# Hybrid attention and HGRN2 encoder layer with MoE: the output projection of a prompt tile issued in sixteen half pieces, and the first mixing tile's operands loaded one stage earlier

## What is computed

```python
h = rmsnorm(x, ln1) * (1 + sc1) + sh1
qa, ka, va, qb, fb, ib, gb = split(h @ w_in)
oa = sliding-window attention(qa, ka, va, sinks)       # 8 heads of 64, 2 key/value heads, window 128, blocks of 64
S, ob = hgrn_scan(S0, qh, kb, ih, logf)                # 8 heads, state 64x64, gated recurrence in blocks
ob = rmsnorm(ob, o_norm) * silu(gb)
x = x + g1 * (concat(oa, ob) @ w_out)                  # output projection, 1024 x 1024
h2 = rmsnorm(x, ln2) * (1 + sc2) + sh2
x = x + g2 * moe(h2)                                   # router, top 2 of 16 experts
```

## Time and profile before

| | |
|---|---|
| median of 3 runs | 1406.37 us (1403.38 to 1411.02) |
| the profiled execution, its own time | 1410.54 us |
| its span, first to last instruction | 1408.5 us |
| mean granted TensorE clock | 0.893 |
| TensorE busy | 1238.9 us, 88% |
| VectorE, ScalarE, GpSimd busy | 737.7, 550.8, 365.7 us |
| mixing stage in the span | 436.8 to 820 us, about |

### The profile page before, as it was taken

How to read it: one execution, slowest core, us unless ns; L and a number is a source line. 1 busy time by engine, 2 the same in 40 slices (tenths; PEclk the granted TensorE clock), 3 DMA queues, 4 the chain that set the end, 5 groups by cost and what they waited for, 6 DMA issues and landing times. The chain is left out here.

```text
span 1408.5 us, 21648 instructions
## 1 busy us (share of the span) xinstructions
PE 1238.9 (88%) x7081; PEld 1022.5 (73%) x7082; DVE 737.7 (52%) x1066; ACT 550.8 (39%) x921; POOL 365.7 (26%) x419
## 2 busy tenths in 40 slices
PE   3789999999595999999999816999999999879964
PEld 1568889988464888888888715788887887668853
DVE  2553510342553666756666466552555585655851
ACT  3363421323322434444444203441444465444640
POOL 1000200122502433433433012233323332433222
PEclk8799999999666998989988956999999999989987
DMA  9626773512256323303321166387759889887864
GB/s 352 215 90 206 253 277 108 162 51 70 70 144 191 102 72 101 102 31 102 102 72 46 34 220 243 135 270 197 249 179 312 275 283 371 268 288 254 268 242 89
DMA packets 119430, 249.87 MB, mean 177 GB/s; under 512 B 17713, under 2 KB 47153, under 8 KB 116290
## 3 DMA queue, kind: packets, MB, share of 16 engines
q1 hardware_dynamic: 107266, 204.92, 41.9%
q0 software_dynamic: 12096, 44.05, 12.0%
HBM read 205.02 MB, written 43.93 MB: 177 GB/s over the span
## 5 line engine op out<-in xcount | busy, mean ns | idle before, releaser
L2106 PE MATMUL psum<-e_w_h,e_x_h 128*128 128x512 f32 x432 | 173.8, 402 | 30.5 <-DVE w_gu L2219 23.7
L2108 PE MATMUL psum<-e_w_h,e_x_l 128*128 128x512 f32 x432 | 171.0, 396 | 0.0
L2107 PE MATMUL psum<-w_gu,e_x_h 128*128 x432 | 170.6, 395 | 0.0
L2053 POOL DMA_INDIRECT out<-e_work,e_to x26 | 87.9, 3380 | 302.1 <-DVE e_work L2207 302.1
L2219 DVE TENSOR_TENSOR w_gu<-w_gu,e_w_h 128x1024 f32 x128 | 146.7, 1217 | 21.1 <-ACT e_w_h L2160 21.1
L2160 ACT ACTIVATE e_w_h<-w_gu 128x1024 fp32r x128 | 123.0, 1048 | 54.5 <-issue 33.3
L2106 PEld LDWEIGHTS psum<-e_w_h,e_x_h 128*128 128x128 f32 x432 | 82.8, 192 | 48.7 <-DVE w_gu L2219 24.1
L498 PE MATMUL psum<-p_w_h,p_h_h 128*128 128x512 f32 (+1 forms) x288 | 107.4, 373 | 1.6 <-DVE p_h_l L653 1.6
L500 PE MATMUL psum<-p_w_h,p_h_l 128*128 128x512 f32 (+1 forms) x288 | 106.8, 371 | 0.0
L499 PE MATMUL psum<-p_w_l,p_h_h 128*128 128x512 f32 (+1 forms) x288 | 106.7, 371 | 0.0
L2108 PEld LDWEIGHTS psum<-e_w_h,e_x_l 128*128 128x128 f32 x432 | 82.5, 191 | 17.8
(11 more groups left out here) (367 smaller groups left out, 2661.5 us busy)
## 6 DMA issues: line engine op xcount, KB each, us to landing
w_gu<-in_w_e_gate SPq DMA_DIRECT2D x16, 2048.0 KB, 15.4
w_gu<-in_w_e_up SPq DMA_DIRECT2D x16, 2048.0 KB, 19.3
w_dn<-in_w_e_down SPq DMA_DIRECT2D x16, 2048.0 KB, 15.5
shared<-in_w_ada SPq DMA_DIRECT2D x24, 1024.0 KB, 6.6
p_w_raw<-in_w_in SPq DMA_DIRECT2D x5, 2048.0 KB, 9.3
m_feat<-feat_d SPq DMA_DIRECT2D x8, 1024.0 KB, 6.6
m_tok<-tok_d SPq DMA_DIRECT2D x8, 896.0 KB, 8.9
tok_d<-p_tok SPq DMA_DIRECT2D x27, 256.0 KB, 2.0
```

The lines of the kernel that those rows point to most:

```text
L2053: pool.indirect_dma_start(out=d["y"], out_offset=bass.IndirectOffsetOnAxis(ap=to_now[1 - par][:, 0:1], axis=0), in_=y_s[:, 1 - par, :], in ...
L2106: pe.matmul(psum[:, j, :], x_h[:, k, :], wh, start=(k == 0), stop=False)
L2107: pe.matmul(psum[:, j, :], x_h[:, k, :], wl, start=False, stop=False)
L2108: last = pe.matmul(psum[:, j, :], x_l[:, k, :], wh, start=False, stop=(k == KC - 1))
```

## The change

1. `fill(u, k)` is cut into `piece(u, k, 0)` and `piece(u, k, 1)`, three matmuls of 512 columns each. In a tile the steps 0 and 1 are still whole; the twelve others are single halves between other steps: two of them now stand in the end of the tile (before and behind `pair`), one between `scores(t, 1)` and level 3, one between the logits and `values(t, 0)`. `values(t, 1)` moves ahead of step 6.
2. `feat` and `tok` have their first buffer (`feat0`, `tok0`) in the memory that lives through both stages; `sampling` loads tile 0 into it, ahead of its wait for the new state. `mixing` no longer does. To make room, `pn_t` and `o_sq` of `sampling` become parts of `cache_t` and `kd_tok`.

```diff
--- before.py
+++ after.py
@@ -167,7 +167,8 @@
             b["w_ol"] = nc.alloc_sbuf_tensor_at("w_ol", [P, KC, D], F32R, offset=low_at)
             b.update(
                 mix_p=sb(mid, "mix_p", [P, 2, KC, P]), w_oh=sb(mid, "w_oh", [P, KC, D], F32R),
-                w_r=sb(mid, "w_r", [P, KC, NE]))
+                w_r=sb(mid, "w_r", [P, KC, NE]), feat0=sb(mid, "feat0", [P, 4, QW]), tok0=sb(mid, "tok0", [P, TOK]),
+                feat0_loaded=sem("feat0_loaded"), tok0_loaded=sem("tok0_loaded"))
             sampling(nc, b, d, sinks, state_in, s_sample)
             mixing(nc, b, d, x, sinks, s_prompt)
         b.update(
@@ -718,6 +719,17 @@
 OUT_A, OUT_B, M0, M1, M2, M3, PJ0, PJ1 = range(8)
 
 
+def load_feat(sp, d, t, feat, loaded):
+
+    sp.dma_start(feat[:, :, :].rearrange("p a (c r) -> p (a c) r", r=P),
+                 d["feat"][:, :, :, t * P:(t + 1) * P].rearrange("p a c r -> p (a c) r")).then_inc(loaded, 16)
+
+
+def load_tok(sp, d, t, tok, loaded):
+
+    sp.dma_start(tok[:, :], d["tok"][t * P:(t + 1) * P, :]).then_inc(loaded, 16)
+
+
 def sampling(nc, b, d, sinks, state_in, s_sample):
 
 
@@ -756,7 +768,7 @@
         top_s, neg_top, sink_e = (sb(n, [P, NKV, BP]) for n in ("top_s", "neg_top", "sink_e"))
         den, rec = sb("den", [P, NKV, BP]), sb("rec", [P, NKV, BP])
         pc_t = sb("pc_t", [P, 8, P])
-        pn_t = sb("pn_t", [L, 8, P])
+        pn_t = cache_t[0:L, :, :]
         o_a = sb("o_a", [P, BP, NKV, HD])
         exp_b, k_d, kd_tok, o_n = (sb(n, [P, QW]) for n in "exp_b k_d kd_tok o_n".split())
         gap = sb("gap", [P, NL, QW])
@@ -769,7 +781,7 @@
         q_m = sb("q_m", [P, 4, NB * (P + L)])
         i_m = sb("i_m", [P, 8, NB, HD])
         new_state = i_m[:, 0:4, :, :]
-        o_sq = sb("o_sq", [P, 8, HD])
+        o_sq = kd_tok[:, :].rearrange("p (h d) -> p h d", d=HD)
         o_ss, o_rs = sb("o_ss", [P, 8]), sb("o_rs", [P, 8])
 
         names = """gate_loaded sink_loaded state_loaded vnew_loaded consts act_chain dve_chain pool_chain
@@ -811,6 +823,8 @@
             for half in (slice(0, D // 2), slice(D // 2, D)):
                 sp.dma_start(d["h2"][ROWS:TABLE, half], zeros[:, :]).then_inc(s["operands_in"], 16)
                 sp.dma_start(d["y"][ROWS:TABLE, half], zeros[:, :]).then_inc(s["operands_in"], 16)
+            load_feat(sp, d, 0, b["feat0"], b["feat0_loaded"])
+            load_tok(sp, d, 0, b["tok0"], b["tok0_loaded"])
             sp.wait_ge(s["state_ready"], 1)
             for n in range(NB):
                 for h in range(2):
@@ -1111,7 +1125,7 @@
 
         w_h, w_l, w_r, mix_p = b["w_oh"], b["w_ol"], b["w_r"], b["mix_p"]
         table = b["shared"][:, :].rearrange("p (a i n) -> p a i n", a=3, i=2)
-        feat, tok = sb("feat", [P, 2, 4, QW]), sb("tok", [P, 2, TOK])
+        feat, tok = (b["feat0"], sb("feat1", [P, 4, QW])), (b["tok0"], sb("tok1", [P, TOK]))
         x_in, x2 = sb("x_in", [P, 2, D]), sb("x2", [P, 2, D])
         xw, h2, h2_t = sb("xw", [P, D]), sb("h2", [P, D]), sb("h2_t", [P, KC, P])
         lhs_h, lhs_l = sb("lhs_h", [P, KC, P], F32R), sb("lhs_l", [P, KC, P], F32R)
@@ -1143,8 +1157,8 @@
             lhs_h_ready lhs_ready lhs_used x1_ready x2_ready squared rs_ready xw_ready h2_ready h2_stored h2_turned h2t_ready
             logit_mm logit_ready""".split()
         s = {n: sem(n) for n in names}
-        feat_loaded, tok_loaded, x_loaded, x2_stored = ([sem(f"{n}{i}") for i in range(2)]
-                                                        for n in ("feat_loaded", "tok_loaded", "x_loaded", "x2_stored"))
+        x_loaded, x2_stored = ([sem(f"{n}{i}") for i in range(2)] for n in ("x_loaded", "x2_stored"))
+        feat_loaded, tok_loaded = (b["feat0_loaded"], sem("feat1_loaded")), (b["tok0_loaded"], sem("tok1_loaded"))
         ctx.callback(retire, nc, sems)
         block = ctx.enter_context(nc.Block())
 
@@ -1166,10 +1180,10 @@
             return mix_p[:, (u + 1) % 2, part, :]
 
         def fts(t, i):
-            return feat[:, t % 2, i, :]
+            return feat[t % 2][:, i, :]
 
         def toks(t, a, n):
-            return tok[:, t % 2, a:a + n]
+            return tok[t % 2][:, a:a + n]
 
         def table_row(i, u):
             return table[:, i, tile_of(u) // TP, :]
@@ -1181,12 +1195,11 @@
                     sp.wait_ge(s["lv_mm"], 2 * NL * (t - 1))
                     sp.wait_ge(s["qe_ready"], t - 1)
                     sp.wait_ge(s["kexp_ready"], t - 1)
-                sp.dma_start(feat[:, t % 2, :, :].rearrange("p a (c r) -> p (a c) r", r=P),
-                             d["feat"][:, :, :, rows(t)].rearrange("p a c r -> p (a c) r")).then_inc(feat_loaded[t % 2], 16)
+                load_feat(sp, d, t, feat[t % 2], feat_loaded[t % 2])
                 if t >= 2:
                     sp.wait_ge(s["ob_ready"], t - 1)
                     sp.wait_ge(s["v_ready"], t - 1)
-                sp.dma_start(tok[:, t % 2, :], d["tok"][rows(t), :]).then_inc(tok_loaded[t % 2], 16)
+                load_tok(sp, d, t, tok[t % 2], tok_loaded[t % 2])
 
             def load_x(u):
                 if u >= 2:
@@ -1201,7 +1214,6 @@
                 sp.wait_ge(s["h2_ready"], u + 1)
                 sp.dma_start(d["h2"][rows(tile_of(u)), :], h2[:, :]).then_inc(s["h2_stored"], 16)
 
-            load_tile(0)
             sp.dma_start(sink[:, :], sinks.partition_broadcast(P)).then_inc(s["sinks_loaded"], 16)
             load_x(0)
             for i in range(3):
@@ -1292,20 +1304,23 @@
                     last = pe.transpose(psum[:, dst, c * P:(c + 1) * P], src[:, c * P:(c + 1) * P], ident[:, :])
                 last.then_inc(done, 1)
 
+            def piece(u, k, n):
+                if n == 0 and k % 4 == 0:
+                    pe.wait_ge(s["lhs_ready"], 2 * u + k // 4 + 1)
+                if n == 0 and k == 0 and u:
+                    pe.wait_ge(s["x1_ready"], u)
+                cols = slice(n * 512, (n + 1) * 512)
+                wh, wl = w_h[:, k, cols], w_l[:, k, cols]
+                out = psum[:, W0 + n, :]
+                pe.matmul(out, lhs_h[:, k, :], wh, start=(k == 0), stop=False)
+                pe.matmul(out, lhs_h[:, k, :], wl, start=False, stop=False)
+                last = pe.matmul(out, lhs_l[:, k, :], wh, start=False, stop=(k == KC - 1))
+                if n == 1 and k % 4 == 3:
+                    last.then_inc(s["lhs_used"], 1)
+
             def fill(u, k):
-                if k % 4 == 0:
-                    pe.wait_ge(s["lhs_ready"], 2 * u + k // 4 + 1)
-                if k == 0 and u:
-                    pe.wait_ge(s["x1_ready"], u)
-                for n in range(2):
-                    cols = slice(n * 512, (n + 1) * 512)
-                    wh, wl = w_h[:, k, cols], w_l[:, k, cols]
-                    out = psum[:, W0 + n, :]
-                    pe.matmul(out, lhs_h[:, k, :], wh, start=(k == 0), stop=False)
-                    pe.matmul(out, lhs_h[:, k, :], wl, start=False, stop=False)
-                    last = pe.matmul(out, lhs_l[:, k, :], wh, start=False, stop=(k == KC - 1))
-                if k % 4 == 3:
-                    last.then_inc(s["lhs_used"], 1)
+                piece(u, k, 0)
+                piece(u, k, 1)
 
             def turn_h2(u):
                 pe.wait_ge(s["h2_ready"], u + 1)
@@ -1389,32 +1404,36 @@
                 fill(t, 0)
                 level(t, 0)
                 fill(t, 1)
-                fill(t, 2)
+                piece(t, 2, 0)
                 level(t, 1)
+                piece(t, 2, 1)
                 turn_probs(t, 0)
-                fill(t, 3)
+                piece(t, 3, 0)
                 if t:
                     turn_ob(t - 1)
                 level(t, 2)
+                piece(t, 3, 1)
                 if t:
                     pe.wait_ge(s["mixb_ready"], t)
                     turn_h2(t - 1)
                 scores(t, 1)
+                piece(t, 4, 0)
                 level(t, 3)
                 if t:
                     logits(t - 1)
-                fill(t, 4)
+                piece(t, 4, 1)
                 values(t, 0)
                 level(t, 4)
+                piece(t, 5, 0)
                 turn_probs(t, 1)
-                fill(t, 5)
+                piece(t, 5, 1)
                 level(t, 5)
-                fill(t, 6)
                 values(t, 1)
+                piece(t, 6, 0)
                 level(t, 6)
                 pe.wait_ge(s["kexp_ready"], t + 1)
                 turn4(OB, k_d, s["kd_turned"])
-                fill(t, 7)
+                piece(t, 6, 1)
                 if t + 1 < TP:
                     turn_qk(t + 1)
                 pe.wait_ge(s["kdt_ready"], t + 1)
@@ -1425,6 +1444,7 @@
                     last = pe.matmul(psum[(h % 2) * HD:(h % 2 + 1) * HD, M1, c * HD:(c + 1) * HD],
                                      kd_tok[:, h * HD:(h + 1) * HD], i_b[:, h * HD:(h + 1) * HD], start=True, stop=True)
                 last.then_inc(s["state_mm"], 1)
+                piece(t, 7, 0)
```

(1 more changed line is left out.)

## The result

The changed kernel takes **1426.19 us** (median of 4 runs, 1425.44 to 1428.98), the kernel before 1404.88 (4 runs, 1399.25 to 1411.02): a ratio of 1.0149, 95% interval 1.012 to 1.0177, or +21 us. The forecast was +7.9 us (1414.3, range 1387 to 1427). The profiled execution took 1428.98 us, with a span of 1427.0.

The account below looks back on a forecast made before the run. TensorE was taken as the bound, at whatever clock it has. Loads -6.1 and half pieces +14.0 (seven tiles +13.5, tile 0 +0.5) gave +7.9 on the 1406.4 us median: 1414.3 us, range 1387 to 1427.

Parts of the forecast that it names:

- Direction: Whole kernel: forecast slower, +7.9 us; chances slower 0.46, same 0.26, faster 0.28.
- Part 1: Tile 0's loads at the mixing stage's start: earlier `feat` and `tok` save 6.1 us, bounds 0 to 8.8.
- GpSimd's chain: Mixing start: iota, two gaps, product, then TensorE's diagonal bring the first `scores` to 442.9 in place of 448.97.
- SyncE's hole: Sample stage, 401.65 to 423.33 us: SyncE has nothing to issue, so both new loads fit at zero cost.
- (b), the middle fall: Between logits and level 5: thinned work drops the clock for 7 to 9 us, 4.0 us lost a tile.
- (b), the end fall: Tile's end: the clock still falls there, low for 7 us, 3.4 us lost a tile.
- (a), the waits: Behind piece 7's last half, 2.9 us later: VectorE delays cost TensorE zero, 1.1 us a tile kept for range.
- The sum of a tile: 37.7 us of work plus 4.0 and 3.4 lost: 45.1 us against 43.2, +1.9 for each of seven tiles.
- Tile 0: First tile, which has no logits: forecast +0.5 us from the half pieces.
- Tile 7 with the closing steps: Last tile: counted among the seven at +1.9 us each.
- rival D: Clock falling in the middle stays low until the next tile's fill 0: 1425 to 1440 us, 8%.
- The page's rule: Clock losses come from TensorE's idle gaps; by it neither order's clock falls in a tile, giving 1376 us.

Follow-up runs that it names:

- the pieces alone: Half pieces put into the kernel before, its loads left where they were: 1436.17 us, ratio 1.0195 to the kernel before.
- both tries on the waits: Changed kernel with GpSimd's `xw` behind its fourth gap: 1439.34 us; changed kernel with VectorE adding x behind the next tile's second `decayed`: 1434.98 us.
- the middle alone: Changed kernel with steps 6 and 7 whole as before, new loads and new middle kept: 1424.42 us, ratio 1.0148 to the kernel before.
- three more matmuls: Changed kernel plus three unused 512-column matmuls between level 3 and the logits in tiles 1 to 7: 1411.54 us, ratio 1.0051 to the kernel before.
- the moved half: Changed kernel with step 4's first half moved from ahead of level 3 to behind the logits: 1399.47 us, ratio 0.9946 to the kernel before.
- the new end alone: Changed kernel with steps 2 to 5 whole as before, new loads and steps 6 and 7 kept: 1398.34 us, ratio 0.9927 to the kernel before.
- the loads alone: Changed kernel with steps 2 to 7 whole in their old places, only the new loads kept: 1398.13 us, ratio 0.9951 to the kernel before.
- the denser middle: Changed kernel with steps 0 to 2 whole, two halves between level 3 and logits, two between logits and values: 1388.49 us, ratio 0.9889 to before.
- both: Changed kernel with the denser middle and VectorE adding x behind the next tile's second `decayed`: 1386.99 us, ratio 0.9873 to the kernel before.

## Why the prediction was right and wrong

**Direction: right, and for the stated reason.** The middle of a tile, thinned, lost the clock between logits and level 5. Counted over tiles 1 to 6 of each profile, this fall stands in 6 of the change, 6 of the pieces alone and of both tries on the waits, 5 of the middle alone; in 2 with three more matmuls, 1 with the half moved back, 1 of the new end alone, 1 of the loads alone, and in none before, with the denser middle, or with both.

**Part 1: right.** -6.1 in the profile by GpSimd's chain, -7 in the runs of the loads alone. The issues sit in SyncE's hole (399.61 and 400.21); the one of `tok` took 4.50 us there, not 2.21, without harm: from the last zeros to the first store of the new state are 21.4 us, before 22.1.

**(b), the middle fall: right in place, a little too small.** "keeps the low clock for 7 to 9 us ... 4.0" lost; it was 10.2 us in four tiles and 6.8 in two, 9.1 in the mean. The tile of 46.74 us, which has this fall alone, has 43.36 of busy time where a tile of the moved half has 38.32 at clock 1.00: 5.0 lost for 10.2 us, of which 4.7 between the steps shown; by its length that makes about 4.4 in the mean.

**(b), the end fall: wrong.** I let it live on, shorter, at 3.4 us a tile. In none of the changed kernel's tiles 1 to 6 does the clock fall at the end, ahead of `scores`. The two halves moved there did more than I gave them, as the new end alone shows. What falls in tiles 2, 4, 5 and 6 falls at the wait for `rest`, 3 to 4.5 us into the tile, a place that the prediction does not have; it is low for 3.4, 3.4, 3.4 and 6.8 us, about 1.4 lost a tile in the mean.

**(a), the waits: the step that failed.** "I take zero and keep 1.1 us a tile for the range. It costs TensorE nothing as long as `scores` and fill 0 cover it". The condition was stated and then kept true by the end fall that I had assumed. With `scores` at 1.99 us the cover is 1.8 us thinner; and the push, forecast at 2.9 us and measured at 3.3, put `rest` and `decayed` beside GpSimd's `xw` and `q_e`, which made them 1.4 and 1.1 us longer. The row was there (the state update at 1.59 us "while GpSimd works"), but I moved only VectorE's operations and left `xw` where it was. Together 1.5 to 3.4 us of waits a tile, 2.2 in the mean, where the sum has zero. That x1 would not be waited for at the turn of `o_a` was right (0.4 us, once, in tile 7).

**The sum of a tile.** TensorE's work at full clock is 38.3 us (the moved half, clock 1.00; 38.2 to 38.5 in the other runs' tiles at 1.00), not 37.7. Of the 0.6, 0.4 lie in two steps that the prediction costed at full clock without a row from that place: `scores` at 1.71 and fill 0 at 1.48, which take 1.99 and 1.59 in tile 1 of the middle alone; the other 0.2 stay open. The mean of tiles 1 to 6 is (758.15 - 480.55) / 6 = 46.3 us. Their mean busy time is 44.1, so that 5.7 are lost to the low clock; shared out by length that is 4.4 in the middle and 1.4 at the wait, and 38.3 + 4.4 + 1.4 + 2.2 = 46.3. The forecast was 37.7 + 4.0 + 3.4 + 0 = 45.1. The waits left out (+2.2) and the end fall kept (-2.0) nearly cancel: that the tile came out only 1.2 us short is luck as far as these two go.

Tile 0 gave +2.3 instead of +0.5: the clock rose 11.9 us behind its first `scores`, before 6.5. That does not go with the order (12.1 in the new end alone, 6.3 in the pieces alone) and stays open. Tile 7 with the closing steps gave +5.4 instead of 1.9, 2.3 of it busy time and 3.1 waits. In all +26.3 where the forecast had +14.0: 7.0 of the 12.3 us from tiles 1 to 6, 1.8 from tile 0, 3.5 from tile 7 and the closing steps. With -6.1 that is +20.2. By its size this is rival D's range, but not its mechanism: the clock was back at full before level 5.

**The page's rule.** By "HAM oscillation" (the Trainium skill, TensorE: Matmul & The Clock Gate) the clock is lost to idle gaps of the engine. The runs show both. With no idle time at all the clock fell twice a tile (47.79 of 47.79 us busy, 0.79). And it fell behind idle gaps: behind a wait of 2.6 us in six tiles of six, behind waits of 2.3 to 3.8 us in five of six. Shorter waits were less clear: behind the 1.2 to 1.7 us for `rest` it fell in four of six tiles of the change and in none with the denser middle. The trace agrees with the rule for what it names; the rule leaves out the narrow work.

**Left open.** Why one order holds the clock in some tiles and loses it in others: the middle alone held it in tile 1 only, the new end alone and the moved half lost it in two tiles of six each. These last two stand near an edge, their runs spread over 13 to 17 us, those of the denser middle over 4. Which of the steps in the middle (16-column logits, 64-column values, 64-row levels) weighs most wasn't tried apart.

## What to carry to other kernels

When TensorE's wide matmuls are what holds its clock, they are a resource to be placed: look at the order for the longest run of narrow steps and put a whole fill in the middle of it, rather than spread halves evenly; here three matmuls in the right place were worth 28 us, and even unused ones more than paid for themselves. Cost a reordering once with the clock that you expect and once with the other one, since faster TensorE takes the cover from VectorE; the waits that come then are cheap while they are short and the clock holds, and dear once it falls behind them.

## What the runs showed that I had not expected

- GpSimd slows VectorE a lot where both read SBUF: `rest` from 0.69 to 2.09 us, `decayed` from 0.42 to 1.50, one of 128x4 from 0.16 to 1.39, each beside a GpSimd multiplication (`xw` or `q_e`), while the `pair` product, which reads PSUM, takes 1.22 us beside `q_e` in the kernel before (577.78) and 1.21 us by itself after (576.70). The slow ones all have two SBUF inputs. That is what GPSIMD Engine Reference in the Trainium skill (section 1, Specifications) says of the SBUF interfaces that it shares with VectorE; the trace agrees, and gives the size.
- Adding 5 us of matmuls made a kernel 14 us faster.
